# Rotary turning in a fused transformer kernel: partner rows copied by ScalarE in place of a product with a rotation matrix

## The reference

```python
def rope(x, pos):                       # first block, all 64 rows of a head
    cos, sin = jnp.cos(ang), jnp.sin(ang)          # ang: position x frequency, 32 of them
    x1, x2 = xf[..., :half], xf[..., half:]
    return jnp.concatenate([x1 * cos - x2 * sin, x2 * cos + x1 * sin], axis=-1)

def apply_partial_rope(x, cos, sin):    # second block, 16 of the 64 rows of a head
    half = ROPE_DIM // 2                # 8
    x1, x2, rest = x[..., :half], x[..., half:ROPE_DIM], x[..., ROPE_DIM:]
    return jnp.concatenate([x1 * c - x2 * s, x2 * c + x1 * s, rest], axis=-1)
```

## Time and profile before

| | us |
|---|---|
| median of 3 runs | 2544.61 (2540.13 to 2551.26) |
| the profiled execution, its own time | 2543.12 |
| its span, first to last instruction | 2541.3 |
| PE busy | 2304.2 (91%) |
| PE loading weights | 1860.0 (73%) |
| DVE busy | 1224.8 (48%) |
| ACT busy | 1037.2 (41%) |
| POOL busy | 663.3 (26%) |
| mean granted clock of PE | 0.936 |

### The profile page before, as it was taken

How to read it: one execution, slowest core, us unless ns; L and a number is a source line. 1 busy time by engine, 2 the same in 40 slices (tenths; PEclk the granted TensorE clock), 3 DMA queues, 4 the chain that set the end, 5 groups by cost and what they waited for, 6 DMA issues and landing times.

```text
span 2541.3 us, 30655 instructions
## 1 busy us (share of the span) xinstructions
PE 2304.2 (91%) x11258; PEld 1860.0 (73%) x11258; DVE 1224.8 (48%) x2264; ACT 1037.2 (41%) x1825; POOL 663.3 (26%) x409
## 2 busy tenths in 40 slices
PE   7987899987999799988988999998996797999997
PEld 6655588866888587766867888886775676788886
DVE  5757444535999634265355322323327545323233
ACT  3435533445888635155253322222126424332221
POOL 4150033311000021500233332332641323233222
PEclk9988899976999899998988999998999998999998
DMA  4200022214999720120121223221220121222221
GB/s 155 100 17 34 9 89 98 100 47 151 380 391 386 294 75 26 67 92 1 67 67 50 99 101 99 92 100 46 88 76 9 50 71 46 76 99 96 95 100 50
DMA packets 71796, 259.57 MB, mean 102 GB/s; under 512 B 7968, under 2 KB 8096, under 8 KB 71264
## 3 DMA queue, kind: packets, MB, share of 16 engines
q1 hardware_dynamic: 66816, 238.89, 26.5%
q0 software_dynamic: 2672, 11.30, 1.2%
q10 hardware_dynamic: 2160, 7.42, 0.8%
HBM read 246.02 MB, written 11.56 MB: 101 GB/s over the span
## 4 chain that ended last, share of the span: by engine, by line
PE 79%; DVE 8%; ACT 4%; issue 4%; POOL 3%; DMA 2%; POOLq 0%; DVEq 0%; SPq 0%; ACTq 0%
PE ps L498 16%; PE ps L499 16%; PE ps L500 16%; PE ps L552 3%; PE ps L1086 2%; PE ps L1070 2%; PE ps L2597 2%; PE ps L2599 2%; PE ps L2598 2%; PE ps L533 2%; PE ps L534 2%; PE ps L535 2%; PE ps L1105 2%; ACT Sb L1179 1%; PE ps L697 1%
## 5 line engine op out<-in xcount | busy, mean ns | idle before, releaser
L440 ACT ACTIVATE wh<-raw 128x1024 fp32r<-128x1024 f32 x308 | 322.5, 1054 | 578.5 <-PE ps L500 550.7
L445 POOL TENSOR_TENSOR wl<-raw,wh 128x1024 fp32r<-128x1024 f32 x128 | 308.9, 2413 | 814.4 <-ACT wh L440 814.4
L445 DVE TENSOR_TENSOR wl<-raw,wh 128x1024 fp32r<-128x1024 f32 x180 | 243.9, 1362 | 544.3 <-ACT wh L440 537.8
L498 PE MATMUL ps<-hh,wh 128*128 128x512 f32 (+1 forms) x1192 | 479.4, 402 | 6.0 <-POOL wl L445 5.6
L500 PE MATMUL ps<-hh,wl 128*128 128x512 f32 (+1 forms) x1192 | 467.4, 392 | 0.0
L499 PE MATMUL ps<-hl,wh 128*128 128x512 f32 (+1 forms) x1192 | 467.1, 392 | 0.0
L498 PE MATMUL ps<-act,wh 128*128 128x512 f32 (+1 forms) x688 | 272.5, 396 | 11.7 <-ACT act L1331 9.9
L499 PE MATMUL ps<-act,wh 128*128 128x512 f32 (+1 forms) x688 | 270.6, 393 | 0.0
L500 PE MATMUL ps<-act,wl 128*128 128x512 f32 (+1 forms) x688 | 269.6, 392 | 0.0
L498 PEld LDWEIGHTS ps<-hh,wh 128*128 128x128 f32 (+1 forms) x1192 | 225.7, 189 | 60.0 <-issue 13.1
L499 PEld LDWEIGHTS ps<-hl,wh 128*128 128x128 f32 (+1 forms) x1192 | 225.6, 189 | 52.0 <-issue 5.9
(11 more groups left out here) (444 smaller groups left out, 3873.4 us busy)
## 6 DMA issues: line engine op xcount, KB each, us to landing
raw<-d_w SPq DMA_DIRECT2D x277, 512.0 KB, 3.5
raw_x<-d_moe SPq DMA_DIRECT2D x84, 512.0 KB, 6.4
raw<-d_moe SPq DMA_DIRECT2D x84, 512.0 KB, 6.5
d_xs<-Sb POOLq DMA_DIRECT2D x7, 514.0 KB, 7.5
Xb<-d_xs ACTq DMA_DIRECT2D x7, 514.0 KB, 6.9
d_ys<-rows ACTq DMA_DIRECT2D x7, 512.0 KB, 6.3
area<-d_mem POOLq DMA_DIRECT2D x3, 1024.0 KB, 5.4
xT<-d_x SPq DMA_DIRECT2D x8, 256.0 KB, 6.4
```

What stands on the lines that cost most here:

```text
L440: me.e.activation(hi, raw, ACT.Copy).then_inc(*me.done("wh", m))
L445: me.e.tensor_tensor(lo, raw, hi.bitcast(F32), ALU.subtract).then_inc(*me.done("wl", m))
L498: me.e.matmul(bank[0:m, 0:n], wh[:, c], hi, start=k == 0, stop=False)
```

## The change

The product with the rotation matrix goes from the 33 turned items of the five places. In its stead ACT copies the four groups of 32 rows of `xh` to the rows of their partners (0 to 31 and 32 to 63 change places, as do 64 to 95 and 96 to 127) into a place of its ring `ta`. DVE multiplies this with the sines in place, POOL multiplies `xh` with the cosines into the destination, and POOL adds. The signs of the turning go into the sine tables through the scale operand of the Sin activation (-1 for the first 32 rows of a head, +1 for the others; not for the table of the latent stage, which keeps its matrix).

In the second block only 16 rows of a head are turned, and their partners lay 8 rows apart. There the columns of the weights are re-ordered on the host (`SPREAD`), so that partners lie 32 rows apart; the frequencies, position codes and compression weights that meet these rows are re-ordered with them. The place in `td` is given back after the cosine product and the copies. The constants `r64` and `rb` go, and a column `sign` comes. PE's loop is one step shorter.

```diff
+SPREAD = (*range(8), *range(16, 40), *range(8, 16), *range(40, 64))
+def spread_cols(a, b):
+    return tuple(h + k for h in range(a, b, 64) for k in SPREAD)
...
-def rotate_pool(K, me, st, n, dst, xn, rows, tb):
-    me.wait_ge("rot", st, n)
+def swap_act(K, me, st, n):
+    i = me.take("ta", "swap", st, n)
+    me.wait_ge("xh", st, n)
+    for r in range(0, 128, 32):
+        at = r + 32 if r % 64 == 0 else r - 32
+        me.e.activation(K.ta[r:r + 32, i, :], K.tdn("xh", st, n)[at:at + 32, :], ACT.Copy).then_inc(*me.done("swap", st, n))
+    me.give("ta", ("swap", st, n), ("tok", st, n))
+
+def swap_dve(K, me, st, n, tb):
+    swapped = K.tan("swap", st, n)
+    me.wait_ge("swap", st, n)
     me.wait_ge("tab", tb)
-    me.e.tensor_tensor(xn, xn, K.tab[0:rows, tb % 4, :], ALU.mult).then_inc(*me.done("cosine", st, n))
+    me.e.tensor_tensor(swapped, swapped, K.tab[:, tb % 4 + 1, :], ALU.mult).then_inc(*me.done("u", st, n))
+
+def swap_pool(K, me, st, n, dst, tb, war):
+    me.wait_ge("xh", st, n)
+    me.wait_ge("tab", tb)
+    for k in war:
+        me.wait_ge(*k)
+    me.e.tensor_tensor(dst, K.tdn("xh", st, n), K.tab[:, tb % 4, :], ALU.mult).then_inc(*me.done("cosine", st, n))
     me.wait_ge("u", st, n)
     me.wait_ge("cosine", st, n)
-    me.e.tensor_tensor(dst, dst, xn, ALU.add).then_inc(*me.done("tok", st, n))
+    me.e.tensor_tensor(dst, dst, K.tan("swap", st, n), ALU.add).then_inc(*me.done("tok", st, n))
...
@@ heads_pe
-    for step in range(n_ + 3):
+    for step in range(n_ + 2):
...
-        n = step - 3
-        if 0 <= n < n_ and items[n]["rope"]:
-            it = items[n]
-            rotate_pe(K, me, st, n, K.tdn("xh", st, n)[0:it["rows"], :], it["rows"], it["rope"][0])
@@ heads_act, behind ahead(K, me, ("L", st, step))
+        n = step - 3
+        if 0 <= n < n_ and items[n]["rope"] is not None:
+            swap_act(K, me, st, n)
@@ heads_dve
-                me.give("td", ("xh", st, n), ("tok", st, n))
+                me.give("td", ("xh", st, n), ("cosine", st, n), ("swap", st, n))
...
-            rotate_dve(K, me, st, n, items[n]["dst"], items[n]["rows"], items[n]["rope"][1], items[n].get("war", ()))
+            swap_dve(K, me, st, n, items[n]["rope"])
@@ angle_table
-            me.e.activation(K.tab[:, tb % 4 + odd, :], r, ACT.Sin).then_inc(*me.done("sine", tb, odd))
+            sign = K.cs("sign") if odd and tb != 2 else 1.0
+            me.e.activation(K.tab[:, tb % 4 + odd, :], r, ACT.Sin, scale=sign).then_inc(*me.done("sine", tb, odd))
@@ diff_tables
-    K.i_dqk = [item(cols(128 * c, 128 * c + 128), a[:, c, :], rope=("rb", 4), war=war) for c in range(16)]
+    K.i_dqk = [item(spread_cols(128 * c, 128 * c + 128), a[:, c, :], rope=4, war=war) for c in range(16)]
```

More of the change, by code:

```diff
@@ L138, in shape_constants @@
     for h0 in (0, 64):
-        inv[h0:h0 + 16, 2] = np.tile(f16, 2)
+        inv[h0:h0 + 8, 2] = inv[h0 + 32:h0 + 40, 2] = f16
     fm = np.zeros((128, 3), np.float32)
@@ L151, in shape_constants @@
     return [("ones", np.ones((128, 128), np.float32)), ("eps", eps), ("root", np.full((128, 1), -0.5, np.float32)), ("ident", ident), ("blk", blk),
-            ("r64", rotation(128, 64, 32)), ("r32", rotation(128, 32, 16)), ("blk4", blk4), ("rb", rotation(128, 64, 8)),
+            ("r32", rotation(128, 32, 16)), ("blk4", blk4), ("sign", np.where(p < 32, -1.0, 1.0).astype(np.float32)[:, None]),
             ("tri", tri), ("cm", cm.reshape(128, NQ * NCMP)), ("inv", inv), ("fm", fm),
@@ L850, in heads_dve @@
                     root_dve(K, me, (st, n), nh=it["norm"][0])
-            if it["rope"]:
+            if it["rope"] is not None:
                 dst = K.td[0:rows, me.take("td", "xh", st, n), :]
@@ L883, in heads_pool @@
         n = step - 3
-        if 0 <= n < n_ and items[n]["rope"]:
+        if 0 <= n < n_ and items[n]["rope"] is not None:
             it = items[n]
-            rotate_pool(K, me, st, n, it["dst"], K.tdn("xh", st, n)[0:it["rows"], :], it["rows"], it["rope"][1])
+            swap_pool(K, me, st, n, it["dst"], it["rope"], it.get("war", ()))
 def values_turn_pe(K, me, st, items, n, ntile):
@@ L1620, in mixer_tables @@
     K.i_idx = [item(cols(A_IW, A_IW + 8) + (None,) * 56 + cols(A_KPE, A_KPE + 32), a[0:96, 19, :], 96, m=96),
-               item(cols(A_IK, A_IK + 64) * 2, a[:, 4, :], rope=("r64", 0))]
-    K.i_idx += [item(cols(A_IQ + 128 * c, A_IQ + 128 * c + 128), a[:, c, :], rope=("r64", 0)) for c in range(4)]
+               item(cols(A_IK, A_IK + 64) * 2, a[:, 4, :], rope=0)]
+    K.i_idx += [item(cols(A_IQ + 128 * c, A_IQ + 128 * c + 128), a[:, c, :], rope=0) for c in range(4)]
     late = K.mis[:, 160:192]
-    K.i_qa = [item(cols(A_Q + 128 * c, A_Q + 128 * c + 128), a[:, 20 + c, :], norm=(2, 64, K.sm("g_q")), rope=("r64", 0),
+    K.i_qa = [item(cols(A_Q + 128 * c, A_Q + 128 * c + 128), a[:, 20 + c, :], norm=(2, 64, K.sm("g_q")), rope=0,
                    late=(late[:, 8 * c:8 * c + 8], 64 ** -0.5)) for c in range(4)]
@@ L1645, in mixer_tables @@
     war = [("end", "pe", "mla_att")]
-    K.i_ka = [item(cols(A_K, A_K + 64) * 2, a[:, 4, :], norm=(2, 64, K.sm("g_k")), rope=("r64", 0), war=war)]
+    K.i_ka = [item(cols(A_K, A_K + 64) * 2, a[:, 4, :], norm=(2, 64, K.sm("g_k")), rope=0, war=war)]
     dv = a[:, 5, 0:256].rearrange("p (i m) -> p i m", i=NQ)
@@ L3005, in even_tables @@
     for c in range(4):
-        cc = cols(E_NQ + 64 * c, E_NQ + 64 * c + 64) + cols(E_NQ + 256 + 64 * c, E_NQ + 256 + 64 * c + 64)
-        K.i_nsa.append(item(cc, a[:, c, :], rope=("rb", 4), war=war))
+        cc = spread_cols(E_NQ + 64 * c, E_NQ + 64 * c + 64) + spread_cols(E_NQ + 256 + 64 * c, E_NQ + 256 + 64 * c + 64)
+        K.i_nsa.append(item(cc, a[:, c, :], rope=4, war=war))
     for c, (o, rp) in enumerate(((E_KC, True), (E_VC, False), (E_KS, True), (E_KW, True))):
-        K.i_nsa.append(item(cols(o, o + 128), a[:, 4 + c, :], rope=("rb", 4) if rp else None, war=war))
+        K.i_nsa.append(item((spread_cols if rp else cols)(o, o + 128), a[:, 4 + c, :], rope=4 if rp else None, war=war))
     vs, vw = by_tile(a[:, 8, :], NQ), by_tile(a[:, 9, :], NQ)
@@ L3801, in pack @@
         if name == "cmp_w1":
-            dst[0:64] = w1[layer][row]
-            dst[64:128] = w1[layer][row]
+            order = range(64) if layer else SPREAD
+            dst[0:64] = w1[layer][row][order, :]
+            dst[64:128] = w1[layer][row][order, :]
             continue
@@ L3808, in pack @@
             w = np.concatenate([a[name][layer][512 + 256 * g + 64 * c:512 + 256 * g + 64 * c + 64] for g in range(2)])
-        if None not in columns and columns[-1] - columns[0] == len(columns) - 1:
+        if columns[0] is not None and columns == cols(columns[0], columns[0] + len(columns)):
             dst[:, 0:len(columns)] = w[:, columns[0]:columns[0] + len(columns)]
```

4 lines of the change are left out of this document (2 added, 2 removed).

## The result

The changed kernel takes 2503.56 us (median of 4 executions, 2502.15 to 2512.53), the kernel before 2542.37 beside it (4 executions, 2538.46 to 2551.26): ratio 0.985, 95% interval 0.9814 to 0.9886. The prediction was 2501, its range 2489 to 2514. The profiled execution has a span of 2502.3 us at a mean granted clock of 0.938 (before: 2541.3 at 0.936). 39.0 us are gone where 42.9 were summed.

The account below looks back on a forecast made before the run. TensorE, with 79% of the chain, was taken as the bound. Gains of 21.8 (dqk), 5.3 (idx), 3.4 (qa), 3.3 (ka) and 9.1 (nsa) sum to 42.9 us, giving 2501 us, range 2489 to 2514.

Parts of the forecast that it names:

- Rival (a): Stage tails keep more: copies take 0.7 us each, VectorE-GpSimd collisions cost in full; gain about 36 us, 2508; chance 0.10.
- idx: Stage with 5 turned items: scoring starts after VectorE's last product, at 55 to 56; gain 5.3 us.
- qa: Stage with 4 turned items before the latent stage: ScalarE is the limit at its end; gain 3.4 us.
- The repeated term: Per turned item in dqk's steady part: without its rotation TensorE saves 0.89 us, 6.34 becoming 5.45; all 33 give 29 us.
- nsa and ka: Stages with 7 and 1 turned items: gains of 9.1 us and 3.3 us from dropped rotations and waits.
- Four copies in 2.25 us: ScalarE's added work per turned item: copies of 32 rows x 512 at 0.54 us each, ends 2.1 and 2.8.
- The third tile of vd: Behind dqk: its half tiles come 10.2 to 11.9 us after the last product, TensorE asks at 10.9; 0.5 off 22.3.
- The meetings: VectorE operations with two SBUF operands beside GpSimd's: about 0.5 us on VectorE and 0.8 on GpSimd each, seemingly shared.
- Rival (b): TensorE's clock moves: one 10 us low-clock stretch more or less is 5 us; 2491 or 2511 with two; chance 0.12.
- (c): Only the steady saving of 29 us comes, tails turning into equal waits elsewhere; 2515; chance 0.06.
- (e): Nothing changes: freed TensorE time is at once waited for elsewhere; 2544; chance 0.03.
- (d): ScalarE becomes the bound above 1.1 us per copy, gain gone at 1.32; at 2 us 2630; chance 0.03.

Follow-up runs that it names:

- The dummy product: Changed kernel plus one unused plain f32 product of constants on TensorE per turned item; 2530.52 us, ratio 0.9918 to the kernel before.
- the variant with the sums of idx: Changed kernel with the sums of idx's turned items and the split of vd's third weight tile moved from GpSimd to VectorE; 2501.1 us, ratio 0.9841.
- The variant with one copy: Changed kernel with a single ScalarE copy of 128 rows in place of four of 32, partner exchange left out; 2499.64 us, ratio 0.9806.
- that with the PSUM operand: Changed kernel, VectorE's sine product reading the item's PSUM bank: without exchange 2502.61 us; with copies written there and vd's third tile split by VectorE 2503.89 us.
- the variant without these meetings: Changed kernel, VectorE's sine product reading the item's PSUM bank instead of the copied rows, exchange left out; 2502.61 us, ratio 0.9805.
- eight copies: Changed kernel with ScalarE's four copies per turn done twice, first into a buffer nobody reads; 2564.0 us, ratio 1.0083 to the kernel before.

## Why the prediction was right, and where its terms were off

*The total.* The sum was too large: 42.9 us, where the places gave 37.7. Rival (a), with 36 and a chance of 0.10, was nearer to the measured gain than the forecast. The time lies within the forecast case (2494 to 2509) because that was wider than the error. What is missing is 1.8 in idx, 1.7 in qa and 1.8 in dqk; the terms below say why.

*The repeated term.* 6.34 to 5.44 us per item, PE's 0.89, and no new bound: right. The dummy product gives it back in nsa and dqk. That nothing is tied to absolute time held as well.

*nsa and ka.* 9.2 for 9.1, and 3.4 for 3.3 with the spread at the low clock in both.

*Four copies in 2.25 us.* Mis-sized: they took 2.59, inside the ends of 2.1 and 2.8. The row at 0.52 was the distance from one activation to a different one that overlaps its tail. Between the pieces here there is no overlap, and the spacing is the length, 0.629, and 0.02 more. Hidden in the steady part, it counts where ScalarE is the limit: qa.

*qa, 1.7 instead of 3.4.* The latent stage's scaling (L1556 before, L1585 now) started 139.08 - 127.95 = 11.1 us behind the column sums that follow qa's products, and starts 134.82 - 126.09 = 8.7 behind them now: 2.4 gained, the copies and the meeting of the last sine product (1.18 us instead of 0.69) being the missing 1.0. The other 0.7 is that this operation itself met GpSimd and took 1.59 us, 0.86 before; as the variant with the sums of idx shows, that loss falls one way or the other at a difference of 0.05 us. The variant with one copy and that with the PSUM operand give 2.9 and 0.5 to 0.9 of it back.

*idx, 3.5 instead of 5.3.* The prediction counted a meeting as 0.5 on VectorE and 0.8 on GpSimd, and put VectorE's last product at 55 to 56, 17.5 to 18.5 us behind the spread at 37.5. VectorE at that place:

```profile
57.44 1.60 DVE L735 TENSOR_TENSOR ta<-ta,tab 128x512 f32<-128x512 f32 x1 [1.47 <-ACT ta L727]
58.96 0.18 DVE L1835 TENSOR_SCALAR mis<-ps 128x32 f32<-128x32 f32 x1
59.18 1.13 DVE L1844 TENSOR_SCALAR sel<-ta,mis 128x256 f32<-128x256 f32 x1
```

The spread is at 38.95 here, so that product begins 18.5 behind it, lasts 1.60 instead of 0.69, and scoring begins 20.2 behind instead of 18; then the scores wait for GpSimd's sums, one in 3.08 us. Taking the meetings away brought the 1.8 us back.

*The third tile of vd.* The step that I sized least well: 0.5 taken off, 2.45 measured (the gap of 2.68 in TensorE's row less the usual 0.23). GpSimd's last sum ended 10.9 us behind the last product of dqk, not 8 to 9.5, for the same reason: its last two operations took 1.75 and 2.10 us instead of 1.29. 22.3 - 2.45 = 19.9, and 20.0 were measured. The variant that moves this one split gained 2.5.

*The meetings.* The prediction said that on a meeting both operations get longer, so that it looks shared, and not like a lock. This is the sentence that the runs refute. In the changed kernel 22 of the 33 sine products start while GpSimd is at work, and each of these lasts what is left of GpSimd's operation plus 0.55 us; the other 11 take 0.64 or 0.69. That gives all 33 lengths to within 0.02 us, from 0.64 to 2.59, and so it does for the 297 products in the nine other profiles that have them: 207 of the 330 were met, and none was shorter than it is alone. Three pairs from the changed kernel, VectorE and then GpSimd:

```profile
1778.36 2.59 DVE L735 TENSOR_TENSOR ta<-ta,tab 128x512 f32<-128x512 f32 x1 [1.03 <-ACT ta L727]
...
1794.67 1.08 DVE L735 TENSOR_TENSOR ta<-ta,tab 128x512 f32<-128x512 f32 x1
...
1800.11 1.71 DVE L735 TENSOR_TENSOR ta<-ta,tab 128x512 f32<-128x512 f32 x1 [3.76 <-ACT ta L727]
```

```profile
1778.00 2.40 POOL L453 TENSOR_TENSOR wl<-raw,wh 128x1024 fp32r<-128x1024 f32 x1
1780.35 1.75 POOL L743 TENSOR_TENSOR area<-td,tab 128x512 f32<-128x512 f32 x1
...
1792.92 2.28 POOL L743 TENSOR_TENSOR area<-td,tab 128x512 f32<-128x512 f32 x1
...
1799.99 1.28 POOL L743 TENSOR_TENSOR area<-td,tab 128x512 f32<-128x512 f32 x1
```

The split ends at 1780.40: 2.04 left, plus 0.55, is the 2.59. The third one: 1801.27 - 1800.11 + 0.55 = 1.71. The operation of GpSimd that begins meanwhile waits in its turn: 1780.35 to the product's end at 1780.95 is 0.6 and its own length 1.2, together near the 1.75. So one at a time, whoever comes first; where the two begin 0.05 us apart, either can get the first turn (above). I had read the pair of the earlier trace rows without looking at what lay ahead of it. It is this, from the kernel before:

```profile
1783.57 1.30 POOL L714 TENSOR_TENSOR td<-td,tab 128x512 f32<-128x512 f32 x1 [1.26 <-PE ps L697]
```

VectorE's split, started at 1784.26, waited for this one to end at 1784.87, and GpSimd's next, started at 1785.01, waited for the split to end at 1785.94. Each got longer because it waited for another. This is what the Trainium skill (SBUF — State Buffer, section "Who interferes with whom") says: an exclusive lock, the loser blocking for the whole instruction. The prediction cited the rule, set it aside, and said that by it the sum would stay within 1 us. But a tail's loss by it is up to the whole other instruction per meeting (2.04 of the 2.40 of a weight's split in the first pair), and not the 0.5 and 0.8 that were taken; the variant without these meetings got 1.8 + 0.5 + 1.0 = 3.3 us back by the places. What kept the error small is that the steady part has cover for all of it: nsa came as predicted, and the step of dqk with it.

*The clock.* Rival (b) had a stretch of 10 us at the low clock at 5 us. Two profiles of the changed kernel differ by 8.5 us, at 0.938 and 0.933. On the mean of the executions the changed kernel's clock (0.9362) is a little above that of before (0.9349), worth 2.6 us, so some of the change in the medians is the clock; no experiment here shows whether the change moves it or chance does.

*The rivals.* (a) had the sizes: its sum was 36 us and 37.5 came at equal clock, its idx 3 (3.5 measured), its qa 1 (1.7), POOL's split for vd 2 to 3 us late (2.45). Its reason was in part another: the copies take 0.63 and not 0.7, and a meeting costs what is left of the other operation. (c) and (e) are out by the five places. (d)'s threshold stood the test with eight copies: the step becomes ScalarE's sum. But its price for the whole kernel was too low in kind: it counted items and not the backlog at the stage's end, which cost 17.07 us at vd alone.

## What to carry to other kernels

Work moved off the engine that sets the pace gave its whole duration back per item here; what it gives back at the ends of the stages depends on the slowest of the engines that took it over, and that is the part to work out operation by operation. When two operations of VectorE and GpSimd are both longer than usual, look at what ran ahead of each before calling it sharing, and look for an operand that can lie in PSUM instead. Where a kernel's executions differ by their clock, compare them at equal clock, or by intervals between events that the edit doesn't move: 5 us in 2500 can be shown so, and not by medians of four to six executions. Equal clock misleads where a kernel waits much more than the others, as the one with eight copies does.

## What the runs showed of the hardware that was not expected

- A VectorE product of two SBUF operands that starts during an operation of GpSimd lasts that one's rest plus 0.55 us, but not less than alone (0.64 to 0.69): 330 products of ten profiles, 207 of them met, to 0.02 us. With one operand in PSUM it took 0.64 to 0.69 in all 66 cases of two profiles, 40 of which began during an operation of GpSimd. A VectorE copy of 32 rows within SBUF, 0.42 alone, lasted GpSimd's rest plus 0.28 us in five cases, up to 1.48.
- Where a VectorE operation began 0.05 us ahead of one of GpSimd, it was held up by it in the changed kernel (1.59 us) and not in the variant with the sums of idx (0.48). What decides it stays open.
- A ScalarE copy of 512 columns costs 0.629, 0.631 or 0.615 us for 32, 64 or 128 rows, moved rows or not, and 0.593 for 32 rows when it writes to PSUM. Four in a row started 0.65 apart (PSUM: 0.62), where two different activations had started 0.52 apart. What decides whether the next one overlaps the last stays open.
- 0.001 of mean granted clock went with 2.0 us of 2500, and executions of one kernel ranged from 0.929 to 0.941 (before).
